# Selection masks split over three engines, a re-ordered sample softmax, and a moved reciprocal in a decoder layer

## The chip, the cores and the metric

The kernel runs on one core of a Trainium2 chip. The metric is the device time of one launch in microseconds (us). The core's engines run beside each other and meet only at semaphores: TensorE (PE in the profile; PEld is its weight loading), VectorE (DVE), ScalarE (ACT), GpSimd (POOL) and SyncE (SP, which only issues DMAs here). Time before: 1739.12 us, the median of 3 runs (1735.95 to 1741.62).

## The reference, cut to what matters

One layer of a decoder for 1024 prompt tokens and 8 sequences of 4 sample tokens, all float32. Mixer A is dilated window attention, mixer B attends to the 256 keys that an indexer picks for each query; then come the output projection, a second normalisation and a SwiGLU FFN.

```python
def select_keys(scores, qpos, topk):            # topk 256 (prompt), 65 (sample)
    causal = jnp.arange(L)[None, :] <= qpos[:, None]
    scores = jnp.where(causal[None], scores, -jnp.inf)
    _, sel = lax.top_k(scores, topk)             # ties: the lowest index first
    return sel, sel <= qpos[None, :, None]
...
    p = jax.nn.softmax(s, axis=-1)               # gathered_attention, mixer B
    o = jnp.einsum('nqkgt,nqtkd->nqkgd', p, vg)
...
def layer_back(x, oa, ob, mods, w_out, norm2_g, w_gate_up, w_down):
    x = x + g1 * (o @ w_out)
    xn = rms_norm(x, norm2_g) * (1 + sc2) + sh2
    gate, up = jnp.split(xn @ w_gate_up, 2, axis=-1)
    return x + g2 * ((jax.nn.silu(gate) * up) @ w_down)
```

## The kernel before

Every engine has its program written out by hand, in four blocks; at a block's end all engines meet, so the engine that ends last sets when the next block starts. Products in float32 are made of three passes over a high and a low part (`gwh`, `gwl` for a weight `gw`; `ahi`, `alo` for an activation): ACT rounds the high part, and POOL or DVE subtracts it for the low one.

**Block 1 (`front`)**: projections of 128-token tiles, on PE. Beside it DVE looks for each query's 256th score by 31 steps of bisection (`count`, `decide`), for six prompt tiles of 384 to 1024 keys (a = 0 to 5) and the sample's 32 x 288 (a = 6). Then `select` makes a tile's mask, 0 where selected and -1e30 elsewhere: `selG` (score above the threshold, with its count), `selE` (equal), a running count of the equal ones in `sig`, `kp` (how many of these are wanted), the equal ones kept (L1466), the sum `selG - 1 + sig` (L1469) and its multiple with 1e30 (L1473, 16 bits for the prompt). POOL's last work there is the low part of the first head's queries and keys (`qst` L1187, `lst` L1190), which PE turns (L693) and ACT copies out (L1043).

**Block 2 (`attention`)**: mixer attention of the prompt, 16 heads.

**Block 3 (`sample_attention`)**: the 32 sample tokens, with sequences in two groups g of four, and x = 0 to 3 for mixer A group 0, A group 1, B group 0, B group 1 (x = g for A, 2 + g for B). PE spreads the sample's mask (L2160) and turns the cached keys `kw` of each sequence n, DVE and ACT copy them, and after each fourth sequence PE makes the scores. Then, one step for all x after another: `smx` and its extreme (L2286, DVE), exponential with row sums `lsum` (L2244, ACT), normalisation by `rsum` (L2290, L2292, DVE), turning (L2203, PE), copies `pT` (L2296, DVE), product with the values `vw` or `vpg` (L2220, PE), picking the head by `headsel` (L2303, L2307, DVE) and a turning product (L2227, PE). SP loads `vw` (8 x 512 KB) after the last `kw`. POOL makes the low part `olo` of the prompt's attention output meanwhile (L2138).

**Block 4 (`back`)**: output projection (L2466), second normalisation in three thirds of 352 tokens (`inverse_root`, `normed`, `normed_low`; ACT makes `ahi`, DVE `alo`), then 11 pairs of FFN slices: `gate_up` (L2489) of two slices f, `down` (L2508). The first `gate_up(0, ...)` takes the thirds as they come; `gate_up(1, ...)` waits for `gwl` of slice 1 (semaphore `gw_lo`).

```python
            for n in range(NSEQ): ...                      # block 3, SP
                sp.dma_start(vw[:, n], ...).then_inc(v_in, 16)
...
            pe.wait_ge(v_in, 16 * NSEQ)                    # block 3, PE
            pe.wait_ge(kv_pg, 2 * 16 * KT * NSEQ)
            pe.wait_ge(pe_, 4)
```

Of the kernel before, what the change touches and what calls it, by code (L numbers as in the profile page):

```python
# [195 lines left out]
def front(nc, A, S):  # L196
# [289 lines left out]
    with nc.Block() as block:  # L486
# [339 lines left out]
        def _(act):  # L826
# [192 lines left out]
            for n in ns:
# [5 lines left out]
                else:  # L1025
# [36 lines left out]
            for a in turns:  # L1062
                ada_bias(a)

        @block.gpsimd
        def _(pool):
# [110 lines left out]
            for q, n in enumerate(ns):  # L1177
                c = proj_no[n]
                for t in range(NTILE + 1):
# [5 lines left out]
                    if u == len(units) - (NTILE + 1) + FIRST_SPLIT_AT:  # L1185
                        pool.wait_ge(S["q_hi"], 1)
# [848 lines left out]
def sample_attention(nc, A, S):  # L2035
# [48 lines left out]
    nr = sem("s_norm_s")  # L2084
# [15 lines left out]
    with nc.Block() as block:  # L2100
# [44 lines left out]
        def _(pe):  # L2145
# [732 lines left out]
```

## Time and profile before

| what | value |
|---|---|
| median of 3 runs | 1739.12 us |
| the profiled execution | 1734.96 us, its span 1733.4 us |
| granted TensorE clock, mean | 0.966 of full speed |
| busy share of the span | PE 92%, DVE 50%, ACT 39%, POOL 35% |
| last work of block 1 | PE 471.87 us, ACT 472.55 us, DVE 478.27 us |
| block 3 | from 784.78 us to 836.08 us |
| block 4's output projection | from 836.55 us |
| first pair's `down` (L2508) | from 998.28 us, PE without a gap from there to 1720.93 us |

A time line's row is: start in us, length in us, engine, line of the kernel, operation, output<-inputs with shapes, how many instructions the row merges (x8), and in brackets how long the engine had been idle before and what ended that. The row of a merged group runs from the first one's start to the last one's end.

### The profile page before, as it was taken

To read this page: it belongs to the slowest core of one execution; us is meant where nothing else is said; L and a number is where in the kernel's file an instruction comes from. 1 tells how busy PE (TensorE), PEld (TensorE's weight loads), DVE (VectorE), ACT (ScalarE), POOL (GpSimd) and SP (SyncE) were. 2 spreads that over 40 slices of the span, in tenths; PEclk is the share of its full clock that TensorE was granted. 3 is DMA by queue.
4 is the path that set the end of the run, shared out by engine and by line. 5 is a ranking of instruction groups with operands and counts; after the bars stand their busy time and mean duration, and the time that the engine had idled before them with its cause. 6 is when DMAs were issued, how large, how long until landed. Compare 5 with 4: busy or idle time off the path is not lost.

```text
span 1733.4 us, 29578 instructions
## 1 busy us (share of the span) xinstructions
PE 1587.4 (92%) x10702; PEld 1485.0 (86%) x10702; DVE 873.5 (50%) x1980; ACT 684.3 (39%) x1788; POOL 605.3 (35%) x758
## 2 busy tenths in 40 slices
PE   4697899999878888886999899999999999999998
PEld 3586688999857777774898899999999999999998
DVE  1804988999958878885215432131330322313315
ACT  4424658788257778773224211112112111020111
POOL 2154167776234324205251423314223233132320
PEclk7799999999979999997999899999999999999999
DMA  8700033535252311007412212111111120111002
GB/s 259 271 25 7 17 111 109 185 111 194 78 160 62 98 37 62 8 1 250 161 37 73 73 37 62 45 28 48 48 49 48 36 60 30 43 48 48 0 1 100
DMA packets 138044, 135.28 MB, mean 78 GB/s; under 512 B 7229, under 2 KB 126957, under 8 KB 137302
## 3 DMA queue, kind: packets, MB, share of 16 engines
q1 hardware_dynamic: 111190, 106.43, 19.5%
q10 hardware_dynamic: 25104, 24.64, 4.4%
q0 software_dynamic: 1648, 2.89, 0.6%
q8 instruction: 58, 0.95, 0.2%
q14 instruction: 44, 0.36, 0.1%
HBM read 115.29 MB, written 27.04 MB: 82 GB/s over the span
## 4 chain that ended last, share of the span: by engine, by line
PE 49%; DVE 2%; ACT 0%; DMA 0%; issue 0%; DVEq 0%; SPq 0%
PE bank L2489 29%; PE wide L2508 15%; PE bank L2466 5%; DVE alo L2756 1%; DMA out_y_p<-yn 0%; DVE xn L2748 0%; DVE rstd L2742 0%; ACT ahi L2600 0%; DVE yn L2817 0%; PE bank L2532 0%; ACT L2576 0%; ACT L2605 0%; DVE x L2720 0%; ACT rstd L2605 0%; DVE x L2797 0%
## 5 line engine op out<-in xcount | busy, mean ns | idle before, releaser
L2712 DVE TENSOR_TENSOR hf<-bank,sg 128x352 f32<-128x352 f32 x66 | 34.6, 525 | 460.6 <-PE bank L2489 447.5
L2669 POOL TENSOR_TENSOR hlo<-hf,hhi 128x352 fp32r<-128x352 f32 x66 | 63.0, 955 | 503.6 <-ACT hhi L2578 503.6
L2489 PE MATMUL bank<-alo,gwh 128*128 128x352 f32 x1056 | 193.9, 326 | 6.9 <-DVE alo L2756 6.9
L2797 DVE SCALAR_TENSOR_TENSOR x<-wide,modT,x 128x352 f32<-128x352 f32 (+1 forms) x264 | 151.3, 573 | 96.8 <-PE wide L2508 96.8
L2489 PE MATMUL bank<-ahi,gwh 128*128 128x352 f32 x1056 | 196.5, 326 | 2.3 <-ACT ahi L2600 1.9
L2489 PE MATMUL bank<-ahi,gwl 128*128 128x352 f32 x1056 | 193.1, 325 | 0.0
L2489 PEld LDWEIGHTS bank<-alo,gwh 128*128 128x128 f32 x1056 | 176.3, 191 | 7.2 <-DVE alo L2756 7.2
L2489 PEld LDWEIGHTS bank<-ahi,gwh 128*128 128x128 f32 x1056 | 175.3, 189 | 6.4 <-ACT ahi L2600 4.8
L2489 PEld LDWEIGHTS bank<-ahi,gwl 128*128 128x128 f32 x1056 | 175.5, 190 | 0.0
L2508 PE MATMUL wide<-hlo,dwh 128*128 128x352 f32 x528 | 171.3, 325 | 0.0
L2576 ACT ACTIVATE sg<-bank 128x352 f32<-128x352 f32 x66 | 30.7, 465 | 354.3 <-PE bank L2489 354.3
L2508 PE MATMUL wide<-hhi,dwl 128*128 128x352 f32 x528 | 170.4, 323 | 0.0
L2508 PE MATMUL wide<-hhi,dwh 128*128 128x352 f32 x528 | 170.0, 322 | 0.0
L2578 ACT ACTIVATE hhi<-hf 128x352 fp32r<-128x352 f32 x66 | 33.0, 500 | 255.7 <-DVE hf L2712 255.7
L2659 POOL TENSOR_TENSOR gwl<-gw,gwh 128x2048 fp32r<-128x2048 f32 x22 | 101.9, 4633 | 48.0 <-ACT gwh L2562 47.9
L1848 PE MATMUL bank<-ident,prob 128*128 128x128 f32 x576 | 97.0, 278 | 17.9 <-DVE pL L1988 16.9
L1988 DVE TENSOR_TENSOR pL<-bank,pH 128x512 fp32r<-128x512 f32 (+1 forms) x192 | 101.4, 551 | 14.5 <-ACT pH L1935 13.1
L1412 DVE TENSOR_SCALAR_CACHE_REDUCE junk<-sig,cand 128x384 uint8<-128x384 f32 (+4 forms) x155 | 106.3, 744 | 0.1
L1960 ACT ACTIVATE prob<-smx,nmax 128x128 f32<-128x128 f32 (+7 forms) x128 | 98.8, 772 | 10.3 <-DVE nmax L2018 9.6
L1935 ACT ACTIVATE pH<-bank 128x512 fp32r<-128x512 f32 (+1 forms) x192 | 90.4, 486 | 25.3 <-PE bank L1848 24.4
L2508 PEld LDWEIGHTS wide<-hhi,dwh 128*128 128x128 f32 x528 | 100.0, 189 | 0.0
L2508 PEld LDWEIGHTS wide<-hlo,dwh 128*128 128x128 f32 x528 | 99.2, 188 | 0.0
(366 smaller groups left out, 3423.1 us busy)
## 6 DMA issues: line engine op xcount, KB each, us to landing
gw<-in_w_gate_up SPq DMA_DIRECT2D x44, 512.0 KB, 5.0
raw<-in_w_ada ACTq DMA_DIRECT2D x14, 1024.0 KB, 8.9
dw<-in_w_down SPq DMA_DIRECT2D x22, 512.0 KB, 3.6
raw<-in_w_ada SPq DMA_DIRECT2D x10, 1024.0 KB, 7.5
raw<-in_w_in ACTq DMA_DIRECT2D x8, 1024.0 KB, 5.7
scr_x<-xT SPq DMA_DIRECT2D x1, 4224.0 KB, 17.5
xnat<-in_x_prompt SPq DMA_DIRECT2D x8, 512.0 KB, 5.6
scr_q<-ubuf SPq DMA_DIRECT2D x32, 128.0 KB, 3.2
```

What stands on the lines that cost most here:

```text
L1412: link(v.tensor_scalar(junk[0:r, joff[a]:joff[a] + w], sig[0:r, o:o + w], cand[0:r, a:a + 1].bitcast(F32), 0.0, ALU.is_ge, ALU.add, accum_ ...
L1848: mm = pe.transpose(dst[:, (j - 4 * b) * P:(j - 4 * b + 1) * P], prob[:, a % RING, j * P:(j + 1) * P], ident[:])
L1935: act.activation(pH[g][:, 4 * b:4 * b + nb, i % 4, :], src[:, 0:nb * P].rearrange("p (j n) -> p j n", n=P), ACT.Copy).then_inc(act_out, 1)
L1960: act.activation(prob[:, m % RING, 0:L], smx[:, m % 2, 0:L], ACT.Exp, scale=-1.0, bias=nmax[:, m % 4:m % 4 + 1], accum_out=rowsum[:, m // ...
L1988: v.tensor_tensor(pL[g][:, 4 * b:4 * b + nb, i % 4, :], src[:, 0:nb * P].rearrange("p (j n) -> p j n", n=P), pH[g][:, 4 * b:4 * b + nb, i ...
L2466: mm = pe.matmul(pb[u % 4][:, 0:THIRD], a[:, d % 2, k, :], b[:, k, third(th)], start=(p == 0 and k == 0), stop=(p == 2 and k == KD - 1))
L2489: mm = pe.matmul(pb[2 * s + side][:, 0:THIRD], a[r][:, k, side, :], b[:, k, third(th)], start=(p == 0 and k == 0), stop=(p == 2 and k == K ...
L2508: mm = pe.matmul(pb[4 + u % 4][:, 0:THIRD], a[:, r, d * P:(d + 1) * P], b[:, r, third(th)], start=(r == 0 and p == 0), stop=(r == 1 and p ...
L2659: pool.tensor_tensor(gwl[r][:], gw[r][:], gwh[r][:].bitcast(F32), ALU.subtract).then_inc(gw_lo, 1)
L2669: pool.tensor_tensor(hlo[:, r, third(th)], hf[:, (3 * r + th) % 2, :], hhi[:, r, third(th)].bitcast(F32), ALU.subtract).then_inc(h_lo, 1)
L2712: v.tensor_tensor(hf[:, s, :], pb[2 * s + 1][:, 0:THIRD], sg[:, s, :], ALU.mult).then_inc(h_mul, 1)
L2797: ins = v.scalar_tensor_tensor(out=x1[:, d, cols], in0=src[:, 0:n], scalar=modT[:, 40 + d, 0:1], in1=x1[:, d, cols], op0=ALU.mult, op1=ALU ...
```

## The change

1. **Selection.** `select` makes `selE` first, then writes the comparison "above the threshold" over the scores `sco`, and computes `kp` after the running count. The sum is left to POOL (`selected`: `sig + sco`, float32), the scaling to ACT (`put_mask`: `1e30 * sig - 1e30`). Three tiles (a = 0, 1, 2) are summed by POOL ahead of its `qst` and `lst`, the four others behind them; ACT writes three masks after its copies of the first head's halves, the four others at its end.
2. **Sample softmax.** The normalisation by `rsum` moves from the probabilities to the output (`scaled`, in the instruction that picks the head). The groups go in the order x = 0, 2, 1, 3; the two of sequences 0 to 3 get their extremes and exponentials between the copies of the later sequences. PE's turning, value products and joining products are issued so that a join stands between value products. The mask is copied by ACT from `wide`, and PE waits for it only at the first scores.
3. **Second normalisation.** `inverse_root(2)` stands ahead of the first third's `hidden` and of `normed_low(1)`; the low part of the second weight slice, `gwl[1]`, is made by DVE after `normed_low(2)` instead of by POOL.

```diff
+            def put_mask(a):
+                r, o, w = (NSAMP if a == 6 else P), ioff[a], width[a]
+                act.wait_ge(pads, 3 + a)
+                dst = mask_sb[:] if a == 6 else mask_b[:, moff[IDXT[a]]:moff[IDXT[a]] + w]
+                act.activation(dst, sig[0:r, o:o + w], ACT.Copy, scale=-NEG, bias=NEG)
...
+                        if u >= len(units) - EARLY_MASKS:
+                            put_mask(u - len(units) + EARLY_MASKS)
...
+            for a in range(EARLY_MASKS, 7):
+                put_mask(a)
...
+            def selected(a):
+                r, o, w = (NSAMP if a == 6 else P), ioff[a], width[a]
+                pool.wait_ge(cand_ready, BITS + 1 + a)
+                pool.tensor_tensor(sig[0:r, o:o + w], sig[0:r, o:o + w], sco[0:r, o:o + w], ALU.add).then_inc(pads, 1)
...
-                link(v.tensor_scalar(selG[0:r, 0:w], sco[0:r, o:o + w], flag[0:r, a:a + 1], 0.0, ALU.is_gt, ALU.add,
-                                     accum_out=cnt[0:r, a:a + 1]))
                 link(v.tensor_scalar(selE[0:r, 0:w], sco[0:r, o:o + w], flag[0:r, a:a + 1], None, ALU.is_equal))
                 joined()
-                link(v.tensor_tensor(kp[0:r, a:a + 1], tk[0:r, 0, a:a + 1], cnt[0:r, a:a + 1], ALU.subtract))
+                link(v.tensor_scalar(sco[0:r, o:o + w], sco[0:r, o:o + w], flag[0:r, a:a + 1], 0.0, ALU.is_gt, ALU.add,
+                                     accum_out=cnt[0:r, a:a + 1]))
                 link(v.tensor_tensor_scan(sig[0:r, o:o + w], selE[0:r, 0:w], selE[0:r, 0:w], 0.0,
                                           ALU.add, ALU.bypass))
                 joined()
-                link(v.scalar_tensor_tensor(out=sig[0:r, o:o + w], in0=sig[0:r, o:o + w], scalar=kp[0:r, a:a + 1],
-                                            in1=selE[0:r, 0:w], op0=ALU.is_le, op1=ALU.mult))
+                link(v.tensor_tensor(kp[0:r, a:a + 1], tk[0:r, 0, a:a + 1], cnt[0:r, a:a + 1], ALU.subtract))
                 joined()
-                link(v.scalar_tensor_tensor(out=sig[0:r, o:o + w], in0=selG[0:r, 0:w], scalar=-1.0,
-                                            in1=sig[0:r, o:o + w], op0=ALU.add, op1=ALU.add))
-                joined()
-                dst = mask_sb[:] if a == 6 else mask_b[:, moff[IDXT[a]]:moff[IDXT[a]] + w]
-                link(v.tensor_scalar(dst, sig[0:r, o:o + w], -NEG, None, ALU.mult))
+                v.scalar_tensor_tensor(out=sig[0:r, o:o + w], in0=sig[0:r, o:o + w], scalar=kp[0:r, a:a + 1],
+                                       in1=selE[0:r, 0:w], op0=ALU.is_le, op1=ALU.mult).then_inc(cand_ready, 1)
+                v.wait_ge(cand_ready, BITS + 1 + a)
...
-            pe.wait_ge(qe, 1)
-            pe.wait_ge(me, 2)
             pe.wait_ge(kv_pg, 16 * KT * NSEQ)
...
+            for q in range(4):
+                turn(q)
+            pe.wait_ge(v_in, 16 * NSEQ)
+            pe.wait_ge(kv_pg, 2 * 16 * KT * NSEQ)
+            weighted(0)
+            weighted(1)
+            weighted(2)
+            join(0)
+            weighted(3)
+            join(1)
+            join(2)
+            join(3)
...
-            for x in range(4):
-                v.wait_ge(ex, x + 1)
-                v.reciprocal(rsum[:, x:x + 1], lsum[:, x:x + 1]).then_inc(rc, 1)
-                v.wait_ge(rc, x + 1)
-                v.tensor_scalar(pr[:, x, :], pr[:, x, :], rsum[:, x:x + 1], None, ALU.mult).then_inc(nr, 1)
...
+                if n in (4, 5):
+                    largest(n - 4)
...
             add_squares(KD - 2)
-            split_gate_up(0, 1)
             pair(0, False)
...
             normed(1, range(KD))
+            v.wait_ge(x1_done, 3 * KD)
+            inverse_root(2)
             hidden(0, 0, True, (0,))
             normed_low(1)
-            v.wait_ge(x1_done, 3 * KD)
-            inverse_root(2)
...
             normed_low(2)
+            v.wait_ge(gw_hi, 2)
+            v.tensor_tensor(gwl[1][:], gw[1][:], gwh[1][:].bitcast(F32), ALU.subtract).then_inc(gw_lo, 1)
```

The instructions as they stand in the engines' rows (the number behind a name tells tensors of one name apart). POOL at the end of block 1, before (`wlo` is a projection weight's low part):

```order
L1125 TENSOR_TENSOR ropeb<-ubuf,rope 32x4x8
L1127 TENSOR_TENSOR ubuf<-ropea,ropeb 32x4x16
L1084 TENSOR_TENSOR wlo<-raw,whi 128x1024 x2
L1187 TENSOR_TENSOR qst_58<-qn_56,qst_58 128x8x64
L1190 TENSOR_TENSOR lst_60<-kn_57,kst_59 128x1024
```

and now:

```order
L1095 TENSOR_TENSOR wlo<-raw,whi 128x1024 x2
L1186 TENSOR_TENSOR sig<-sig,sco 128x384
L1186 TENSOR_TENSOR sig<-sig,sco 128x512
L1186 TENSOR_TENSOR sig<-sig,sco 128x640
L1205 TENSOR_TENSOR qst_58<-qn_56,qst_58 128x8x64
L1208 TENSOR_TENSOR lst_60<-kn_57,kst_59 128x1024
L1186 TENSOR_TENSOR sig<-sig,sco 128x768
L1186 TENSOR_TENSOR sig<-sig,sco 128x896
L1186 TENSOR_TENSOR sig<-sig,sco 128x1024
L1186 TENSOR_TENSOR sig<-sig,sco 32x288
```

Seven sums are new; four stand behind `lst`, last on POOL in this block. DVE in the second normalisation of block 4, before (`rstd` is the root's inverse, `xn` the scaled input):

```order
L2742 RECIPROCAL rstd_13618<-rstd_13618 128x352
L2748 SCALAR_TENSOR_TENSOR xn_13609<-x_13611,sc_13605,rstd_13618 128x352 x8
L2712 TENSOR_TENSOR hf<-bank,sg 128x352
L2756 SCALAR_TENSOR_TENSOR alo<-xn_13609,modT,ahi 128x352 x8
L2742 RECIPROCAL rstd_13618<-rstd_13618 128x352
L2773 TENSOR_TENSOR xn_13609<-x_13611,rstd_13618 128x8x32
L2776 TENSOR_TENSOR xn_13609<-xn_13609,sc_13605 128x8x32
L2779 TENSOR_TENSOR xn_13609<-xn_13609,modT 128x8x32
L2748 SCALAR_TENSOR_TENSOR xn_13609<-x_13611,sc_13605,rstd_13618 128x320 x8
L2783 TENSOR_TENSOR alo<-xn_13609,ahi 128x8x32
L2756 SCALAR_TENSOR_TENSOR alo<-xn_13609,modT,ahi 128x320 x8
```

and now:

```order
L2799 RECIPROCAL rstd_13632<-rstd_13632 128x352
L2805 SCALAR_TENSOR_TENSOR xn_13623<-x_13625,sc_13619,rstd_13632 128x352 x8
L2799 RECIPROCAL rstd_13632<-rstd_13632 128x352
L2769 TENSOR_TENSOR hf<-bank,sg 128x352
L2813 SCALAR_TENSOR_TENSOR alo<-xn_13623,modT,ahi 128x352 x8
L2830 TENSOR_TENSOR xn_13623<-x_13625,rstd_13632 128x8x32
L2833 TENSOR_TENSOR xn_13623<-xn_13623,sc_13619 128x8x32
L2836 TENSOR_TENSOR xn_13623<-xn_13623,modT 128x8x32
L2805 SCALAR_TENSOR_TENSOR xn_13623<-x_13625,sc_13619,rstd_13632 128x320 x8
L2840 TENSOR_TENSOR alo<-xn_13623,ahi 128x8x32
L2813 SCALAR_TENSOR_TENSOR alo<-xn_13623,modT,ahi 128x320 x8
L2844 TENSOR_TENSOR gwl_13631<-gw_13629,gwh_13630 128x2048
```

The third third's reciprocal stands before the `hf` of the first third, and `gwl` is DVE's last instruction of the normalisation.

## Rows read from the trace of the kernel before

**Rows 1.** DVE time line, selection's end: start us, us, instruction, [idle before <-releaser].

```profile
461.68 2.01 DVE L1466 SCALAR_TENSOR_TENSOR sig<-sig,kp,selE 128x896 f32<-128x896 f32 x1
463.72 3.17 DVE L1469 SCALAR_TENSOR_TENSOR sig<-selG,sig 128x896 f32<-128x896 f32 x1
...
473.28 1.22 DVE L1469 SCALAR_TENSOR_TENSOR sig<-selG,sig 128x1024 f32<-128x1024 f32 x1
...
477.97 0.30 DVE L1473 TENSOR_SCALAR mask_sb<-sig 32x288 f32<-32x288 f32 x1
```

**Rows 2.** Groups by line, 0 to 620 us (busy us, mean ns | idle).

```profile
L1469 DVE SCALAR_TENSOR_TENSOR sig<-selG,sig 128x384 f32<-128x384 f32 (+6 forms) x7 | 7.9, 1124 | 0.2
...
L1473 DVE TENSOR_SCALAR mask_b<-sig 128x384 bf16<-128x384 f32 (+5 forms) x6 | 3.2, 527 | 0.2
...
L1462 DVE TENSOR_TENSOR kp<-tk,cnt 128x1 f32<-128x1 f32 (+1 forms) x7 | 1.1, 158 | 0.2
...
L1784 POOL TENSOR_TENSOR lst<-kn,kst 128x1024 fp32r<-128x1024 f32 x8 | 19.1, 2384 | 0.0
```

**Rows 3.** POOL time line, 440 to 480 us.

```profile
460.90 1.83 POOL L1187 TENSOR_TENSOR qst<-qn,qst 128x512 fp32r<-128x512 f32 x1 [23.69 <-ACT qst L1047]
462.69 3.24 POOL L1190 TENSOR_TENSOR lst<-kn,kst 128x1024 fp32r<-128x1024 f32 x1
```

**Rows 4.** ACT time line, 466 to 482 us.

```profile
471.47 1.08 ACT L1043 ACTIVATE kL<-bank 128x512 fp32r<-128x512 f32 x2 [0.20 <-PE bank L693]
```

**Rows 5.** PE time line, sample stage.

```profile
790.78 1.94 PE L2175 MATMUL bank<-ident,kw 128*128 128x128 f32 x8 [2.31 <-DMA vpg<-in_cache_v]
...
818.52 1.54 PE L2203 MATMUL bank<-ident,pr_s 128*128 128x128 f32 x6 [6.53 <-DVE pr_s L2292]
...
822.98 3.29 PE L2220 MATMUL wide<-vw,pT_s 128*32 128x512 f32 x16 [0.90 <-DVE pT_s L2297]
...
831.88 3.74 PE L2227 MATMUL bank<-pick,ob_s 128*128 128x16 f32 x32
```

**Rows 6.** DVE time line, sample stage.

```profile
789.87 0.81 DVE L2271 COPY mask_s<-bank 128x288 f32<-128x288 f32 x2
...
813.38 5.09 DVE L2292 TENSOR_SCALAR pr_s<-pr_s,rsum_s 128x288 f32<-128x288 f32 x1
```

**Rows 7.** Instructions of tile `vw`: count, ns, first and last start; time to landing.

```profile
L2116 SPq DMA_DIRECT2D vw<-in_state_win_v x8: 469/478/824, 803.8 to 807.6; - x8
...
DMA to landing us min/median/max: 5.2/8.8/12.1
```

**Rows 8.** Chain that ended last: start us, us, what.

```profile
951.17 8.97 DVE alo L2756 x8
...
960.18 6.05 PE bank L2489 x19
```

**Rows 9.** DVE time line, second normalisation.

```profile
937.54 4.05 DVE L2756 SCALAR_TENSOR_TENSOR alo<-xn,modT,ahi 128x352 fp32r<-128x352 f32 x8
...
950.73 0.53 DVE L2712 TENSOR_TENSOR hf<-bank,sg 128x352 f32<-128x352 f32 x1 [2.79 <-ACT sg L2576]
...
960.05 2.34 DVE L2742 RECIPROCAL rstd<-rstd 128x352 f32<-128x352 f32 x1
```

**Rows 10.** PE time line, second normalisation.

```profile
974.84 1.46 PE L2489 MATMUL bank<-ahi,gwh 128*128 128x352 f32 x8
```

**Rows 11.** POOL time line, sample stage and second normalisation.

```profile
804.05 14.24 POOL L2138 TENSOR_TENSOR olo<-oT,ahi 128x352 fp32r<-128x352 f32 x16
...
953.68 4.90 POOL L2659 TENSOR_TENSOR gwl<-gw,gwh 128x2048 fp32r<-128x2048 f32 x1 [31.64 <-ACT gwh L2562]
958.54 1.20 POOL L2669 TENSOR_TENSOR hlo<-hf,hhi 128x352 fp32r<-128x352 f32 x1
```

**Rows 12.** Busy us of PE, PEld, DVE, ACT, POOL; granted PE clock, DMA, GB/s.

```profile
824.00:826.00 2.00, 2.00 (x16) 0.26 (x7) 0.00 (x0) 0.04 (x1) 2.00 (x2) 0.55 0.00 0
...
963.00:966.00 3.00, 3.00 (x11) 2.55 (x10) 2.97 (x8) 2.15 (x5) 0.00 (x0) 0.54 0.18 44
```

More of the change, by code:

```diff
@@ L1185, in _ @@
                     if u == len(units) - (NTILE + 1) + FIRST_SPLIT_AT:
+                        for a in range(EARLY_MASKS):
+                            selected(a)
                         pool.wait_ge(S["q_hi"], 1)
@@ L1192, in _ @@
                                            ALU.subtract).then_inc(S["k_lo"], 1)
+            for a in range(EARLY_MASKS, 7):
+                selected(a)
         @block.vector
@@ L2194, in _, with turn @@
                 mm.then_inc(sc, 1)
-            for x in range(4):
-                pe.wait_ge(nr, x + 1)
-                b = bank[x % 2] if x % 2 == 0 else bank[2]
-                if x >= 2:
-                    pe.wait_ge(pe_, x - 1)
+            def turn(q):
+                x = ORDER[q]
+                pe.wait_ge(ex, q + 1)
+                b = bank[2 * (q % 2)]
+                if q >= 2:
+                    pe.wait_ge(pe_, q - 1)
                 for a in range(3):
@@ L2221, in _, with join @@
                 mm.then_inc(om, 1)
-            for x in range(4):
-                pe.wait_ge(oe, x + 1)
+            def join(q):
+                x = ORDER[q]
+                pe.wait_ge(oe, q + 1)
                 for c in range(4):
@@ L2229, in _, with exponential @@
                                    start=True, stop=True)
-            mm.then_inc(xt, 1)
+                if q == 3:
+                    mm.then_inc(xt, 1)
+            for q in range(4):
[10 more added lines that the diff above has]
+            join(3)
         @block.scalar
         def _(act):
+            def exponential(q):
+                x = ORDER[q]
+                act.wait_ge(mx, q + 1)
+                act.activation(pr[:, x, :], smx[:, x, :], ACT.Exp, scale=-1.0, bias=nmax[:, x:x + 1],
+                               accum_out=lsum[:, x:x + 1]).then_inc(ex, 1)
+            for g in range(2):
+                act.wait_ge(mm_m, g + 1)
+                act.activation(mask[:, 2 + g, :], wide[g][:, 0:NEWW], ACT.Copy).then_inc(me, 1)
             for n in range(NSEQ):
@@ L2268, in _, with largest, place, scaled @@
             last.then_inc(ke, 1)
-            for g in range(2):
-                v.wait_ge(mm_m, g + 1)
-                v.tensor_copy(mask[:, 2 + g, :], bank[2 + g][:, 0:NEWW]).then_inc(me, 1)
+            def largest(q):
+                x = ORDER[q]
+                g, c0 = x % 2, 512 * (x // 2)
+                v.wait_ge(sc, 1 + g)
+                if q == 0:
+                    v.wait_ge(ldc, NCONST)
+                    v.wait_ge(small_in, 64)
+                    v.wait_ge(me, 2)
+                v.tensor_tensor_reduce(smx[:, x, :], wide[g][:, c0:c0 + NEWW], mask[:, x, :], -(HD ** -0.5), 3e38,
+                                       ALU.add, ALU.min, nmax[:, x:x + 1]).then_inc(mx, 1)
+            def place(q):
+                x = ORDER[q]
+                v.wait_ge(pt, q + 1)
+                b = bank[2 * (q % 2)]
+                v.tensor_copy(pT[:, x, 0:2, :], b[:, 0:256].rearrange("p (a n) -> p a n", a=2))
+                v.tensor_copy(pT[0:NSAMP, x, 2, :], b[0:NSAMP, 256:384]).then_inc(pe_, 1)
+            def scaled(q):
+                x = ORDER[q]
+                g = x % 2
+                v.wait_ge(rc, 1)
+                v.wait_ge(om, q + 1)
+                if x < 2:
+                    src = wide[g][:, 0:512].rearrange("p (h d) -> p h d", d=HD)
+                    out = ob[:, x, :].rearrange("p (h d) -> p h d", d=HD)
+                    heads = headsel[:].unsqueeze(2).to_broadcast([P, 8, HD])
+                    v.scalar_tensor_tensor(out=out, in0=src, scalar=rsum[:, x:x + 1], in1=heads,
+                                           op0=ALU.mult, op1=ALU.mult).then_inc(oe, 1)
+                else:
+                    for a in range(2):
+                        src = wide[g][:, 512 + HD * a:512 + HD * a + HD].unsqueeze(1).to_broadcast([P, 4, HD])
+                        out = ob[:, x, 256 * a:256 * a + 256].rearrange("p (h d) -> p h d", h=4)
+                        heads = headsel[:, 4 * a:4 * a + 4].unsqueeze(2).to_broadcast([P, 4, HD])
+                        last = v.scalar_tensor_tensor(out=out, in0=src, scalar=rsum[:, x:x + 1], in1=heads,
+                                                      op0=ALU.mult, op1=ALU.mult)
+                    last.then_inc(oe, 1)
             for n in range(NSEQ):
```

62 lines of the change are left out of this document (24 added, 38 removed).

## The prediction

> **What bounds the kernel now.** I read the chain that ended last first. From 836.55 us on it is PE nearly all the way, apart from one stretch: eight DVE instructions at 951.17, 8.97 us long, and then PE's gate products at a slow pace [rows 8]. From 998.28 us to the end PE has no gap, so nothing in the last 735 us can be gained or lost by this change, except at the very start of that stretch. The chain does not show what lies before 836.55, since the four blocks are joined by meetings of all engines; there the time lines at each block's end say who came last. Block 1 ends with DVE at 478.27 us, with the sample's mask [rows 1], some 6 us behind PE and ACT; ACT's last copies end at 472.55 [rows 4]. Block 3 ends with PE's joining product at 835.62 [rows 5], and inside it PE stood 6.53 us before the turning of the probabilities, for DVE's normalisation [rows 5]. So there are three places, and each is worked out from its own rows.
>
> **Part 1, selection.** DVE loses the seven sums of L1469 (7.9 us), the six multiples of L1473 (3.2) and the sample's (0.3): 11.4 us [rows 1, 2]. The seven subtractions of L1462 (1.1 us in all) used to run beside the running count and now stand alone between two waits; I take 0.9. DVE by itself would be done at 478.27 - 11.4 + 0.9 = 467.8. But the block then ends with those who got the work. POOL's price: 2384 ns for 1024 columns [rows 2] is 2.33 ns a column, so 0.9, 1.2 and 1.5 us for the early sums, which fall into POOL's idle time of 23.69 us before `qst` [rows 3], and 1.8, 2.1, 2.4 and 0.7 (7.0 together) for those behind `lst`. ACT's price: two copies of 512 in 1.08 us [rows 4], about 1.05 ns a column, so 3.8 us for the five masks that follow its last copies.
>
> What matters is that the two engines hinder each other. L1466 ended at 463.69, 0.96 us after POOL's `qst` (462.73); L1469 at 466.89, again 0.96 us after POOL's `lst` (465.93); the `lst` itself took 3.24 us instead of 2.38 [rows 1 to 3]. An instruction with two tensors in SBUF on DVE and one on POOL take turns, whole instruction by whole instruction. And turns are not fair: the normalisation of 288 columns at 813.38 lasted 5.09 us, to the end of POOL's sixteen back-to-back subtractions at 818.29 [rows 6, 11]. The Trainium skill ("SBUF — State Buffer", Who interferes with whom) says the same of the port pair that VectorE and GpSimd share: it is locked, and whoever comes second fully blocks until the first instruction ends. The trace agrees, by the two ends 0.96 us behind POOL's.
>
> If they ran freely, POOL would be done at 465.9 + 7.0 = 472.9 and ACT at 472.6 + 3.8 = 476.4: a gain of 1.9. With turns: POOL goes through `lst` and the sums of 768 and 896 columns to about 470.8 while DVE's work on the 1024 tile stands still; DVE needs 1.3 us more for it (1.22 at this width [rows 1]), the 1024 sum takes 2.4 after the sample's comparison (0.3), DVE's sample tile ends 1.5 later, then the last sum (0.7) and mask (0.3), with about 0.4 of semaphores: 477.7. I take that: -0.6 us. Bounds: -1.9 (free) and +1.5 (POOL gets in only when DVE is through at 467.8, pays `qst` and `lst` as well, 1.2 + 2.4 + 7.0 + 0.3, to 478.7, and loses a little more in turns).
>
> **Part 2, sample softmax.** The mask copies (0.81 us, ending at 790.68) leave DVE, and PE's wait before the first `kw` turns ended 0.1 us behind them (the bracket names a DMA, which came earlier) [rows 5, 6]. ACT has nothing else to do there. The loads of later `kw` wait for these turns, so the whole series moves by 0.8, as does SP's list behind it. PE was through with the scores at 818.52 - 6.53 = 811.99, now 811.2. The stall on DVE's 5.09 us goes: DVE writes only PSUM copies there, of the kind that ran beside POOL without loss, and by about 815 all four are turned. What is late next is `vw`: the last of eight loads was issued at 807.6 and the longest landing is 12.1 us [rows 7], 819.7, or 818.9 after the shift. So the value products start at about 818.9 instead of 822.98: -4.0 us. From there PE has the same instructions, 822.98 to 835.62 = 12.6 us; a join costs 3.74 / 4 = 0.9, so joins 1 and 2 cover the scaling of the last output, now two instructions. The reordering among them is worth nothing, as PE waits for none of them.
>
> One price comes back. PE will have idled 4 us before the value products and starts them at the lower of its two clock levels (1.2 GHz). Before, it was there until about 825.8 (0.55 granted in 824 to 826), 2.8 us of that work; after the gap at 960.18 it lasted until about 965.8 (0.54 in 963 to 966), 5.6 us [rows 8, 12]. Half of the difference is lost: 0 to 1.4, I take 0.8. Sum of part 2: -3.2; bounds -4.1 (no loss) and -1.9 (`vw` no earlier, full loss).
>
> **Part 3, second normalisation.** The eight `alo` of the second third took 8.97 us, the same eight of the first 4.05 [rows 8, 9]: the 4.92 lost are POOL's `gwl`, 4.90 us from 953.68 [rows 11]. That POOL work goes. In front of the eight now stands the third reciprocal, 2.34 us, but DVE idled 2.79 there [rows 9]; since it needs ACT's third root, I expect `hf` 0.6 later. What POOL does next, `hlo` (1.2 at most [rows 11], take 1.0), still cuts in: 951.8 + 4.05 + 1.0 = 956.9 instead of 960.14. PE goes on 3.2 earlier, still slow, and the reciprocal no longer stands before the third third. POOL's `dwl` (1024 columns, 2.4) now falls among the third's `alo`, so these end about 968.5, and PE's first slice ends after two more passes at 971.2 (before: 974.84, when the second slice began [rows 10]). DVE's `gwl` of 2048 columns is not in the trace: twice the 1.22 of 1024 [rows 1] is 2.4, to 970.9, and the `hf` behind it frees PE's bank at 971.4. So the second slice starts at about 971.3: -3.5 us. Bounds: -6.3 if PE doesn't fall to the lower clock in the shorter gap and `dwl` comes elsewhere; -1.5 if `gwl` has to wait for one more POOL instruction and PE for it.
>
> **Sum.** -0.6 - 3.2 - 3.5 = -7.3 us. The profiled execution took 1734.96 (span 1733.4), so it would be 1727.7; the median of the three runs stands 4.2 above it, and the forecast is 1739.1 - 7.3 = 1731.8. The difference is 0.42%; what a measurement of this kernel can tell from no change is about 0.3%, 5.2 us.
>
> **Rivals.**
> *Turns eat the gain.* Part 1 ends at its upper bound (+1.5), and in part 3 DVE's new `gwl` loses its turn (-1.5): 1739.1 + 1.5 - 3.2 - 1.5 = 1735.9. For it: the 5.09 us. Against it: DVE's two-tensor work gets shorter in all three places.
> *The loads are the wall.* `w_out`'s two loads are now issued earlier too, behind `vw`; should they share its bandwidth, `vw` lands 2 to 3 us later and part 2 shrinks to -0.6: 1734.4. For it: eight loads landed one after the other in 5.2 to 12.1 us. Against it: they were issued before `vw` was in already, and it still landed by 819.7.
> *More than forecast.* No fall of the clock in part 3, free running in part 1: 1739.1 - 1.9 - 4.1 - 6.3 = 1726.8.
> *Slower: the clock does not come back.* Place: the value products and the first gate products. If PE, after its gaps, stays at 1.2 GHz for as long as the work behind them is broken up by waits, the 9.8 us that ran fast at the end of block 3 (825.8 to 835.6) double, and block 3 ends at 818.9 + 2.8 + 19.6 = 841.3, 5.7 later than before; and the 64 gate products still to come at 956.9 take 6.05 / 19 = 0.318 us each [rows 8], to 977.3, 2.4 later. With part 1: 1739.1 - 0.6 + 5.7 + 2.4 = 1746.6. It decides from the point where the clock is not up by about 831 and 968. For it: the clock stayed down 5.6 us after 960.18. Against it: both times it rose while PE had work without gaps, as it has in the new order.
> *The change doesn't do what it says*: nothing in the order speaks for it.
>
> **How the numbers follow.** Forecast 0.55, more than forecast 0.10, turns 0.15, loads 0.12, clock 0.08. The first two are faster by over 0.3%: 0.65; turns and loads lie within: 0.27; the clock case slower: 0.08. The likeliest case's own range is 1728 to 1735. The range holds the two on the fast side and the two within, with the spread of the three runs at the edges: 1725 to 1738.5.
>
> **What would show it.** Right: block 1 ends with ACT's sample mask, after POOL's last sum, 0 to 2 us before 478.3; PE's first value product waits for `vw`, at 818 to 820, less part 1's gain; no POOL `gwl` beside the second third's `alo`, which take about 5 us; the second slice of `gate_up` starts some 7 us earlier in the span. Wrong: DVE still last in block 1; a value product that waits for `pT`; DVE's `gwl` over 4 us; a stretch of `down` later than 993.

## The result and the profile after

The changed kernel took 1728.78 us (median of six runs, 1725.88 to 1730.94) against 1738.82 us for the kernel before in the same session (six runs, 1735.95 to 1741.62). The ratio is 0.9943, 95% interval 0.9932 to 0.9954: 10.0 us less, between 8.0 and 11.8. Forecast were 7.3 us less. Direction and range held; the three terms of the sum did not, as the rest shows.

The profiled execution of the changed kernel has a span of 1729.3 us, only 4.1 less than the 1733.4 of before: the execution profiled was the slowest of its six (1730.94 us), that of before (1734.96) faster than all six of its own. So I cut both spans at the same instructions: first comparison of the selection, first memset of block 2, first memset of block 3, first `vw` product, first output projection product, first `down` product (before: at 998.12 us; 998.28 is its second), last `down` product, end. The kernel before was profiled a second time for this (see the experiments). All in us, from the time lines:

| stretch | before | before, 2nd profile | after |
|---|---|---|---|
| start to selection | 438.19 | 437.43 | 438.07 |
| selection to block 2 | 41.00 | 41.01 | 41.58 |
| block 2 | 305.59 | 305.52 | 305.73 |
| block 3 to the first `vw` product | 38.19 | 38.20 | 34.01 |
| that product to the output projection | 13.57 | 16.53 | 16.72 |
| output projection to `down` | 161.57 | 161.55 | 156.39 |
| `down` to the last product | 722.80 | 722.80 | 722.80 |
| tail | 12.53 | 12.54 | 14.01 |

Three stretches that differ repeat to 0.02 us in the two profiles of before, and belong to the change: +0.6, -4.2, -5.2, together -8.8. The profiles of the experiments bear the first two out to about 0.2 us (but for the one that moves the loads). The third is less firm: 161.55 to 163.14 us in five profiles with the old second normalisation, 155.70 to 157.15 in seven with the whole new one. The stretch behind the first `vw` product is a matter of the execution: 13.6 or 16.5 us in the *same* kernel. Whether the tail is one too is not shown: it is 13.7 to 14.1 us in four of the six profiles that have parts 2 and 3 together, 12.5 in the other two and in all eight without.

**Selection.** VectorE's time line of the changed kernel (start us, us, instruction): comparisons `selE`, and one that also writes its count.

```profile
440.90 1.34 DVE L1478 TENSOR_SCALAR selE<-sco,flag 128x512 f32<-128x512 f32 x1
...
445.18 1.68 DVE L1478 TENSOR_SCALAR selE<-sco,flag 128x640 f32<-128x640 f32 x1
...
450.34 2.02 DVE L1478 TENSOR_SCALAR selE<-sco,flag 128x768 f32<-128x768 f32 x1
...
456.37 0.69 DVE L1478 TENSOR_SCALAR selE<-sco,flag 128x896 f32<-128x896 f32 x1
...
463.30 1.28 DVE L1480 TENSOR_SCALAR_CACHE_REDUCE sco<-sco,flag 128x1024 f32<-128x1024 f32 x1
...
472.48 2.55 DVE L1478 TENSOR_SCALAR selE<-sco,flag 32x288 f32<-32x288 f32 x1
```

GpSimd's time line there (in brackets the idle time before and who ended it).

```profile
440.94 1.01 POOL L1186 TENSOR_TENSOR sig<-sig,sco 128x384 f32<-128x384 f32 x1 [3.87 <-DVE sig L1487]
445.22 1.29 POOL L1186 TENSOR_TENSOR sig<-sig,sco 128x512 f32<-128x512 f32 x1 [3.27 <-DVE sig L1487]
450.38 1.56 POOL L1186 TENSOR_TENSOR sig<-sig,sco 128x640 f32<-128x640 f32 x1 [3.87 <-DVE sig L1487]
...
465.49 5.88 POOL L1186 TENSOR_TENSOR sig<-sig,sco 128x768 f32<-128x768 f32 x2
472.53 2.35 POOL L1186 TENSOR_TENSOR sig<-sig,sco 128x1024 f32<-128x1024 f32 x1 [1.16 <-DVE sig L1487]
477.05 0.78 POOL L1186 TENSOR_TENSOR sig<-sig,sco 32x288 f32<-32x288 f32 x1 [2.18 <-DVE sig L1487]
479.65 0.20 POOL L1768 MEMSET pH<- 128x128 f32 x1 [1.82 <-POOLq L487]
```

The comparison of 768 columns took 2.02 us with a sum beside it, that of 896 columns 0.69 us with none: each of the three early sums starts 0.04 us behind a comparison, and the comparison ends 0.3 to 0.4 us behind the sum. The prediction had charged turns only to instructions with two tensors in SBUF; this one has one. The Trainium skill ("SBUF — State Buffer", Who interferes with whom) names it: tensor_scalar can take the shared port pair, but not in the form that also writes its accumulator. The trace agrees in both: the counting comparison of 1024 columns beside `lst` took 1.28 us, as in kernels without these sums. Where the Trainium skill there lets whoever issues first go first, the rows show the sum going first though by its row the comparison began 0.04 us earlier.

Beside the late sums VectorE's tile of 1024 columns went slowly: its scan, `kp` and kept equals had taken 2.28, 0.16 and 1.29 us before.

```profile
464.50 3.17 DVE L1482 TENSOR_TENSOR_SCAN sig<-selE 128x1024 f32<-128x1024 f32 x1
467.71 1.63 DVE L1485 TENSOR_TENSOR kp<-tk,cnt 128x1 f32<-128x1 f32 x1
469.37 3.08 DVE L1487 SCALAR_TENSOR_TENSOR sig<-sig,kp,selE 128x1024 f32<-128x1024 f32 x1
```

The last mask comes where the prediction had it, on ACT after the last sum:

```profile
477.86 0.44 ACT L1021 ACTIVATE mask_sb<-sig 32x288 f32<-32x288 f32 x1 [1.90 <-POOL sig L1186]
```

That ends at 478.30, before at 478.27 [rows 1]. But block 2 starts 1.35 us later, not 0.92 as before: the row at 479.65 waited for GpSimd's own sequencer. The instructions at the meeting's line (count, duration ns min/median/max, first and last start) show why: GpSimd's closing DRAIN began at 477.0 and lasted to 479.4, 1.6 us past the end of its last sum.

```profile
L487 POOLq DRAIN  x1: 2385/2385/2385, 477.0 to 477.0; - x1
...
L487 ACTq DRAIN  x1: 459/459/459, 477.9 to 477.9; - x1
```

In the kernel before GpSimd's DRAIN ended as long behind its last work (`lst`, 465.93 us), but far ahead of the meeting, where it cost nothing:

```profile
L486 POOLq DRAIN  x1: 5697/5697/5697, 461.8 to 461.8; - x1
```

**Sample softmax.** PE's time line of the changed kernel, which answers to [rows 5]:

```profile
790.68 1.73 PE L2189 MATMUL bank<-ident,kw 128*128 128x128 f32 x7 [3.25 <-DMA vpg<-in_cache_v]
...
812.95 1.05 PE L2220 MATMUL bank<-ident,pr_s 128*128 128x128 f32 x6 [0.77 <-DVE pT_s L2326]
819.39 3.64 PE L2237 MATMUL wide<-vw,pT_s 128*32 128x512 f32 x16 [5.39 <-DMA vw<-in_state_win_v]
...
826.41 3.08 PE L2237 MATMUL wide<-vw,pT_s 128*32 128x512 f32 x16
```

The wait for DVE's normalisation (6.53 us) is gone, and PE stands before `vw` instead. The value products then run slowly: 3.64 us for 16, which at the higher clock level take 1.92 (in the experiments below). Busy us of PE, PEld, DVE, ACT, POOL, then granted clock, DMA share, GB/s of the changed kernel:

```profile
820.00:828.00 8.00, 8.00 (x56) 1.78 (x52) 1.62 (x3) 2.11 (x2) 4.66 (x2) 0.50 0.10 25
828.00:836.00 8.00, 7.19 (x76) 4.60 (x68) 2.05 (x4) 0.07 (x1) 0.00 (x0) 0.93 0.00 0
```

PE was at its lower level (1.2 GHz) through 8 us without a gap.

**Second normalisation.** VectorE's time line, which answers to [rows 9]:

```profile
948.60 2.35 DVE L2799 RECIPROCAL rstd<-rstd 128x352 f32<-128x352 f32 x1 [1.07 <-ACT rstd L2663]
950.98 0.52 DVE L2769 TENSOR_TENSOR hf<-bank,sg 128x352 f32<-128x352 f32 x1
951.42 4.73 DVE L2813 SCALAR_TENSOR_TENSOR alo<-xn,modT,ahi 128x352 fp32r<-128x352 f32 x8
...
961.36 3.79 DVE L2813 SCALAR_TENSOR_TENSOR alo<-xn,modT,ahi 128x320 fp32r<-128x320 f32 x8
965.07 2.28 DVE L2844 TENSOR_TENSOR gwl<-gw,gwh 128x2048 fp32r<-128x2048 f32 x1
```

GpSimd's, which answers to [rows 11]:

```profile
952.12 1.18 POOL L2727 TENSOR_TENSOR hlo<-hf,hhi 128x352 fp32r<-128x352 f32 x1 [30.50 <-ACT hhi L2636]
962.73 6.89 POOL L2721 TENSOR_TENSOR dwl<-dw,dwh 128x1024 fp32r<-128x1024 f32 x1 [9.44 <-ACT dwh L2626]
```

PE's, which answers to [rows 8, 10]:

```profile
956.21 5.06 PE L2547 MATMUL bank<-alo,gwh 128*128 128x352 f32 x16 [3.41 <-DVE alo L2813]
...
966.63 2.75 PE L2547 MATMUL bank<-alo,gwh 128*128 128x352 f32 x16
969.22 1.46 PE L2547 MATMUL bank<-ahi,gwh 128*128 128x352 f32 x8
```

`alo` of the second third takes 4.73 us instead of 8.97; the second slice starts 5.6 us earlier in the span, 5.2 counted from the output projection: 3.5 of these are the second third's `alo`, 1.7 come behind them. What was to cut into the third third's `alo`, GpSimd's `dwl`, did not: it was the one that waited, 6.89 us, until VectorE's series of eight and the `gwl` behind it were through. PE comes to the third third's `alo` at 966.63, 1.5 us after they are done, and from 956.21 on it waits for nothing. The profile of before had shown `dwl` waiting there already (GpSimd's time line), beside a series of eight that took 3.78 us:

```profile
969.09 4.69 POOL L2663 TENSOR_TENSOR dwl<-dw,dwh 128x1024 fp32r<-128x1024 f32 x1 [9.34 <-ACT dwh L2568]
```

### The profile page after: what moved, and what is told of

It reads as the page before. It is cut to its first block, busy times and chain, and to the rows that moved or that the text cites. A ratio compares the mean times of both kernels' runs of the same rounds, so it can differ in the third digit from the quotient of the medians.

```text
span 1729.3 us, 29588 instructions
## 1 busy us (share of the span) xinstructions
PE 1583.8 (92%) x10702; PEld 1481.2 (86%) x10702; DVE 863.5 (50%) x1960; ACT 688.4 (40%) x1797; POOL 614.5 (36%) x764
## 4 chain that ended last, share of the span: by engine, by line
PE 49%; DVE 1%; DMA 0%; ACT 0%; issue 0%; DVEq 0%; SPq 0%
PE bank L2547 29%; PE wide L2566 15%; PE bank L2524 5%; DVE alo L2813 0%; DMA out_y_p<-yn 0%; DVE rstd L2799 0%; DVE xn L2805 0%; ACT ahi L2658 0%; DVE yn L2876 0%; PE bank L2590 0%; ACT L2663 0%; DVE x L2777 0%; ACT rstd L2663 0%; DVE x L2856 0%; DVE hf L2769 0%
## 5 line engine op out<-in xcount | busy, mean ns | idle before, releaser
L2717 POOL TENSOR_TENSOR gwl<-gw,gwh 128x2048 fp32r<-128x2048 f32 x21 | 97.0, 4619 | 16.4 <-ACT gwh L2620 16.4
L2566 PEld LDWEIGHTS wide<-hhi,dwl 128*128 128x128 f32 x528 | 99.2, 188 | 0.0
```

The source lines that it names most:

```text
L2566: mm = pe.matmul(pb[4 + u % 4][:, 0:THIRD], a[:, r, d * P:(d + 1) * P], b[:, r, third(th)], start=(r == 0 and p == 0), stop=(r == 1 and p ...
L2717: pool.tensor_tensor(gwl[r][:], gw[r][:], gwh[r][:].bitcast(F32), ALU.subtract).then_inc(gw_lo, 1)
```

## The experiments

Each gives the median, the change against the kernel before with its 95% interval, and the stretches of the profile. The change is worked out from the ratio of the runs (the kernel before took 1737.8 to 1739.2 us), and can differ from the difference of two medians by some 2 us.

**One part alone.** The diff of one part applied to the kernel before; its core is in the change above.

> The kernel before with the first part alone (selections written over the scores, sums on GpSimd, 16-bit masks from ScalarE). Theory A (each part is worth what the trace of the changed kernel shows at its place): the first block ends where it did, since GpSimd's three early sums hold VectorE's next comparison up by 0.7 to 1.3 us each; the time is 0.0 to +0.6 us against the kernel before, inside its spread. Theory B (the sums of the forecast): -0.6 us. Rival C (the medians differ by 10.0 us and the traced steps explain 6 to 7, so the first part is worth the rest): -3 to -4 us.

Measured: 1740.53 us, ratio 1.001 (1.0001 to 1.0019): +1.7 us (0.2 to 3.3). Selection 41.58, as in the changed kernel. Theory A is the nearest; B and C fall. The first part does not help; it costs, 0.6 us at its place and at least 0.2 in the whole.

> The kernel before with the second part alone (sample softmax: pipelined by pairs, normalisation folded into the last product). Theory A (the first value product starts when vw has landed, about 3.6 us earlier, but TensorE runs at 1.2 GHz for some 9 us behind the wait instead of 3): the stretch from the block's start to the output projection is 50.7 us long, -1.0 us. Theory B (forecast): the clock is back as fast as before, -3.2 us; the first value product waits for vw in both. Rival C: without the first part's shift the loads land at another time against the scores, and the clock comes back at once: -4 us.

Measured: 1733.36 us, 0.9967 (0.9956 to 0.9979): -5.7 us (-7.7 to -3.7). First `vw` product 34.02 us into the block (-4.2), then 13.92 to the output projection: the loss that theory A took from the profile after belongs to that execution. The clock was back 3.3 us behind the first product here, as theory B has it. A and B fall as sizes; C's size came nearest, but not for its reason (GpSimd's and SP's loads landed where they did).

> The kernel before with the third part alone (second normalisation: reciprocal of the second third before the first product of the feed-forward, last gwl on VectorE). Theory A: -5.2 to -5.6 us, all of it there when the first down product starts (second third's alo beside an idle GpSimd, 4.7 us instead of 9.0). Theory B (forecast): -3.5 us. Rival C: part of it is given back at the end of the program, where the last two stores have to land: -4 us, with the last stores landing in over 4 us.

Measured: 1733.57 us, 0.9968 (0.9955 to 0.9981): -5.6 us (-7.8 to -3.3). Output projection to `down` 157.15 instead of 161.57, although 5.4 us of the projection ran at 1.2 GHz in this execution. Theory A; C falls, the tail is 12.54 us as before.

> The changed kernel with the first part undone (selection as in the kernel before). Theory A (the first part is worth nothing or costs 0.5 us): the time is that of the changed kernel or up to 0.5 us less, -10 us against the kernel before. Theory B (forecast): 0.6 us slower than the changed kernel. Rival C (the first part carries what the trace does not explain): 3 to 4 us slower than the changed kernel, about -6.5 us against the kernel before.

Measured: 1727.01 us, 0.9935 (0.9921 to 0.9949): -11.3 us (-13.7 to -8.9). Selection is 41.00 again, the rest 33.81, 13.80 and 156.39. Theory A: without its first part the change is at least as good. Its interval overlaps that of the whole change; that it is better is shown only by way of the first part's own +1.7.

**Does PE's wait set the clock?** In parts 2 and 3:

```diff
             for q in range(4):
                 turn(q)
+            for i in range(36):
+                pe.transpose(bank[1][:, (i % 2) * P:(i % 2 + 1) * P], ident[:], ident[:])
             pe.wait_ge(v_in, 16 * NSEQ)
```

> Parts 2 and 3, and 36 turns of the identity into a free bank on TensorE while it waits for vw (after the last weights are turned, before the wait). Theory A (block 3 differs between executions, 47.6 to 50.7 us, by how long TensorE stays at 1.2 GHz behind its wait for vw): with no wait of over 1 us ahead of it the granted clock is 1.00 through the value products, the first 16 vw products take 1.9 us instead of 3.4, and block 3 is 45.5 to 46.5 us long, 1.5 us less than the shortest seen; time -12 to -13 us against the kernel before. Rival (the low stretch has its cause in something else, such as the loads at that time or the 32-column products): the clock falls at 815 as before, and nothing or a loss of up to 0.5 us.

Measured: 1727.04 us, 0.9935 (0.9921 to 0.9948): -11.3 us, as without the turns. PE's time line, first in parts 2 and 3 without the turns, then with them:

```profile
819.18 3.42 PE L2221 MATMUL wide<-vw,pT_s 128*32 128x512 f32 x16 [5.35 <-DMA vw<-in_state_win_v]
...
829.21 2.85 PE L2229 MATMUL bank<-pick,ob_s 128*128 128x16 f32 x24
```

```profile
819.32 1.92 PE L2221 MATMUL wide<-vw,pT_s 128*32 128x512 f32 x16 [1.69 <-DMA vw<-in_state_win_v]
...
827.85 4.57 PE L2229 MATMUL bank<-pick,ob_s 128*128 128x16 f32 x24
```

The slow products do come of the wait: with 1.69 us of it left, the first 16 took 1.92 us, as expected; the next run shows the same without turns. But then the clock fell with PE at work (windows of the same run, columns as above):

```profile
820.00:828.00 8.00, 8.00 (x102) 3.02 (x94) 2.38 (x4) 2.11 (x2) 4.68 (x2) 1.00 0.10 25
828.00:836.00 8.00, 7.08 (x33) 7.00 (x34) 3.95 (x11) 2.82 (x8) 0.00 (x0) 0.54 0.23 62
```

The idle 0.92 us in it are the meeting at the block's end. The last joins took 4.57 instead of 2.85 us, and the projection's start ran slowly. The gain of 1.5 us was given back at once; theory A had this half wrong.

**Is `vw`'s landing the wall?** In parts 2 and 3:

```diff
+            for n in range(3):
+                load_values(n)
             for n in range(3, NSEQ):
                 load_window(n)
-            for n in range(NSEQ):
+            for n in range(3, NSEQ):
+                load_values(n)
```

> Parts 2 and 3, and the first three vw loads issued ahead of the fourth kw load, where the loading queue waits for a free kw buffer. Theory A (the landing of vw is the wall of block 3, and the DMA engines had room from 788 to 797): vw has landed by 815 to 816 instead of 818.9, the first value product starts there, the wait is under 2.5 us, and the clock stays up or falls for less: -3 to -5 us against parts 2 and 3, -14 to -16 against the kernel before. Rival (the loads as a whole are the wall: what vw gains kw loses): the last kw lands 2 to 4 us later, the scores end that much later, and the time is that of parts 2 and 3 within 1 us.

Measured: 1728.55 us, 0.995 (0.9931 to 0.9969): -8.7 us (-12.0 to -5.4), no better than without; in the profile the first `vw` product comes 35.17 us into the block instead of 33.81. PE's time line:

```profile
800.41 1.97 PE L2178 MATMUL bank<-ident,kw 128*128 128x128 f32 x8 [4.76 <-DMA kw<-in_state_win_k]
...
819.72 1.92 PE L2226 MATMUL wide<-vw,pT_s 128*32 128x512 f32 x16 [0.88 <-DMA vw<-in_state_win_v]
...
828.26 4.86 PE L2234 MATMUL bank<-pick,ob_s 128*128 128x16 f32 x24
```

The wait moved from `vw` to `kw`; the first value product came no earlier, and behind the short wait the products were fast and the joins slow, as with the turns. The rival comes nearest, but the scores ended 5.8 us later where it had 2 to 4, with a loss of 1.4. That the loads as a whole are the wall is not shown: from 802.84 to 807.97 SyncE issued nothing, since it waited for PE's turns to free a `kw` buffer, and the DMA engines were partly idle (windows, columns as above):

```profile
804.00:807.00 3.00, 3.00 (x43) 1.35 (x33) 0.00 (x0) 0.00 (x0) 3.00 (x4) 0.85 0.62 188
807.00:810.00 3.00, 2.56 (x22) 2.14 (x21) 2.62 (x7) 2.11 (x5) 3.00 (x4) 1.00 0.30 64
```

An order of loads that fills this room was not tried.

**The first part without GpSimd.** On the first part alone:

```diff
-                pool.tensor_tensor(sig[0:r, o:o + w], sig[0:r, o:o + w], sco[0:r, o:o + w], ALU.add).then_inc(pads, 1)
...
                 v.wait_ge(cand_ready, BITS + 1 + a)
+                v.tensor_tensor(sig[0:r, o:o + w], sig[0:r, o:o + w], sco[0:r, o:o + w], ALU.add).then_inc(pads, 1)
```

> The first part with the sums left on VectorE: selections written over the scores, 16-bit masks from ScalarE, nothing added to GpSimd; parts 2 and 3 undone. Theory A (the first part loses what it saves to GpSimd's turns at the port: comparisons of 0.5 to 0.6 us that took 1.3 to 2.0): VectorE's comparisons take 0.48 to 0.62 us again, the seven scalings (3.5 us) are gone, selection ends 2 to 3 us earlier than in the kernel before, less 0.4 us at the block's end that falls on ScalarE; -2 to -3 us. Rival (ScalarE's masks or the end of the block on ScalarE hold it up, not the port): no gain, 0 to +1 us.

VectorE's time line: the comparison that took 1.68 us beside a sum.

```profile
445.56 0.55 DVE L1469 TENSOR_SCALAR selE<-sco,flag 128x640 f32<-128x640 f32 x1
```

Selection to block 2 takes 38.17 us instead of 41.00, and block 2 starts 0.26 us behind ACT's last mask. So 3.4 us between this form and the change's are GpSimd's sums: theory A at its place. They are not lost at the early sums alone: VectorE comes to the tile of 1024 columns at 461.61 us in the changed kernel and at 463.04 here, where it makes the sums itself. The time does not show the gain: 1738.01 us, 0.9999 (0.999 to 1.0009). The other stretches of its profile (305.72, 38.20, 16.48, 161.84) are those of before's second profile. Why the median stays is open.

**The third part, halved.** The reciprocal alone:

```diff
+            v.wait_ge(x1_done, 3 * KD)
+            inverse_root(2)
             hidden(0, 0, True, (0,))
             normed_low(1)
-            v.wait_ge(x1_done, 3 * KD)
-            inverse_root(2)
```

> The third part without its second edit: the reciprocal of the last third moved ahead of the first product, the last gwl left on GpSimd. Theory A (what counts is that GpSimd's gwl no longer lies beside alo of the second third): alo of the second third still takes 8 to 9 us, and the move of the reciprocal gives only what its place is worth; -1 us, from -2 to 0. Rival (the earlier reciprocal lets ScalarE and VectorE run ahead, and is worth most of the 5.2 us): -4 to -5 us.

Measured: 1736.95 us, 0.9988 (0.9979 to 0.9997): -2.1 us (-3.7 to -0.5); projection to `down` 159.85. Theory A, just past its lower end. `alo` is still held by GpSimd's `gwl` (VectorE's row of its time line):

```profile
955.51 8.96 DVE L2756 SCALAR_TENSOR_TENSOR alo<-xn,modT,ahi 128x352 fp32r<-128x352 f32 x8
```

The other half, `gwl` on VectorE alone, without its twin on GpSimd:

```diff
             normed_low(2)
+            v.wait_ge(gw_hi, 2)
+            v.tensor_tensor(gwl[1][:], gw[1][:], gwh[1][:].bitcast(F32), ALU.subtract).then_inc(gw_lo, 1)
```

> The third part without its first edit: the last gwl on VectorE, the reciprocal of the last third where it was. Theory A (the two edits add up: both 5.2 us, the reciprocal alone about 2): alo of the second third takes 4.7 us instead of 9.0, the reciprocal of the last third (2.35 us) follows it, and the time is -3 us, from -4 to -2. Rival (the reciprocal behind alo puts the last third so late that VectorE's own gwl, 2.3 us, is what TensorE waits for): -1 us or less.

Measured: 1734.37 us, 0.9982 (0.9969 to 0.9995): -3.1 us (-5.4 to -0.9); projection to `down` 159.18. Theory A; within their intervals the halves add up, -2.1 and -3.1 to the measured -5.6. By the stretches they are -1.7 and -2.4, 4.1 of the 5.2.

```profile
952.73 4.74 DVE L2755 SCALAR_TENSOR_TENSOR alo<-xn,modT,ahi 128x352 fp32r<-128x352 f32 x8
```

**The kernel before, again**, unchanged.

> The kernel before, unchanged, for a second profile. Theory A (its first profiled execution, 1734.96 us, was a lucky one: block 3 took 51.8 us there and 54.3 to 54.7 in all four profiles of other kernels with the old sample softmax): block 3 takes about 54.4 us, TensorE is at 1.2 GHz from 815 to about 828 and again at the start of the output projection, and the execution is 1737 to 1740 us. Rival (the first profile was typical, and the other kernels' edits lengthen block 3): block 3 takes 51.8 us.

Its execution took 1738.25 us. Theory A: 16.53 us behind the first `vw` product. Windows (columns as above):

```profile
820.00:828.00 8.00, 7.10 (x34) 1.75 (x37) 1.62 (x6) 2.12 (x2) 4.67 (x2) 0.50 0.06 14
828.00:836.00 8.00, 8.00 (x90) 3.60 (x82) 2.50 (x4) 0.00 (x0) 0.00 (x0) 0.80 0.01 2
```

Over all profiles with the old sample softmax this stretch is 13.57 us once and 16.16 to 16.53 six times.

**Towards a better version.** Parts 2 and 3 with the first part in its form without GpSimd (diff above):

> Parts 2 and 3 with the first part in its form without GpSimd (sums on VectorE, masks from ScalarE). Theory A (the 2.3 us by which the second block starts earlier in the trace of that form stay to the end): -13.5 us against the kernel before. Rival (what is gained ahead of block 3 is lost there, since its loads or TensorE's clock then fall differently, as the median of that form alone suggests): -11.3 us, that of parts 2 and 3.

Measured: 1725.78 us, 0.9943 (0.992 to 0.9965): -9.9 us (-13.9 to -6.1). The profiled execution is theory A in each stretch (38.26, 33.91, 13.65, 156.49; span 1722.9), but two of the six runs took 1733 and 1735. The lowest median, undecided by its interval.

Then nine output buffers (VectorE's half; ACT's and SP's lines change alike):

```diff
-                if t >= 3:
-                    v.wait_ge(y_out[t % 3], 16 * (t // 3))
-                v.tensor_copy(yn[0:rows, t % 3, 512:1024], pb[2 * (t % 2) + 1][0:rows, :]).then_inc(y_ev2, 1)
+                v.tensor_copy(yn[0:rows, t, 512:1024], pb[2 * (t % 2) + 1][0:rows, :]).then_inc(y_ev2, 1)
```

> The same, and nine output buffers in place of three, over tiles that are done with by then, so that no copy of the output waits for a store. Theory A (the tail's two waits for stores, 2.7 and 3.0 to 4.8 us, are what lies between the last product and the last store): another -3 to -5 us, from the last product to the last store's issue 5 to 7 us instead of 9.7 to 11.5. Rival (the stores come out at the rate of the queue, and the last one lands as late): 0 to -1 us.

Measured: 1730.56 us, 0.9947 (0.993 to 0.9963): -9.2 us. The last store is issued 7.9 us behind the last product instead of 11.1 in the run before (9.7 in the kernel before), but landed 5.3 us after its issue, not 1.9 (2.2): tail 13.92 us against 13.70, no gain, the rival. This profile also shows the clock of the prediction's slower rival, though not its condition, waits between the products. PE's time line, without a gap from 816.51 to the block's end at 837.68:

```profile
816.51 3.64 PE L2229 MATMUL wide<-vw,pT_s 128*32 128x512 f32 x16 [5.58 <-DMA vw<-in_state_win_v]
...
832.38 5.30 PE L2237 MATMUL bank<-pick,ob_s 128*128 128x16 f32 x24
```

Its windows (columns as above): 1.2 GHz throughout, and the stretch is 22.09 us, 8.4 more than in the run before.

```profile
820.00:828.00 8.00, 8.00 (x60) 1.78 (x56) 1.63 (x3) 0.78 (x1) 4.06 (x2) 0.50 0.01 2
828.00:836.00 8.00, 8.00 (x57) 6.20 (x50) 1.63 (x3) 0.00 (x0) 0.00 (x0) 0.50 0.00 0
```

## Why the prediction was right, and where not

*Part 1: -0.6 forecast, +0.6 at its place, +1.7 (0.2 to 3.3) alone; the sign was wrong.* The last mask was to end at 477.7 and ended at 478.30, and the block ended 0.43 us later still. Two steps failed. I put the early sums into GpSimd's idle time as if they cost VectorE nothing, since I took a comparison with one tensor for free of turns; each held up the next comparison, by 0.9, 1.1 and 1.4 us (1.34, 1.68 and 2.02 against 0.48, 0.55 and 0.61 in the form without GpSimd). A row that I used said otherwise: the normalisation of 5.09 us [rows 6] has the comparison's form, one tensor and a scalar for each partition. How much of these 3.4 us reaches the block's end no run shows. And I ended the block with the last mask; it ends when GpSimd's sequencer has drained, 1.6 us past its last instruction. The times of the late sums came right (VectorE's work on the tile of 1024 columns ended at 472.45, 472.1 forecast), but in part by luck: VectorE did not stand still until GpSimd was through. Its scan went in between `lst` and the sum of 768 columns, which took 3.83 us instead of 1.8.

*Part 2: -3.2 forecast, -5.7 (-7.7 to -3.7) alone.* Its first step held: `vw` bounds, at 819.39 in the changed kernel; -4.0 forecast, -4.2 measured, -4.0 to -4.4 in all six profiles with this order of loads. The step that failed is the price of 0.8 us for the clock, taken as a property of the kernel. It is one of the execution: 13.6 to 16.7 us behind the first product in both kernels, once 22. The execution of before that I worked from was the shortest of seven; the new form was at 13.65 to 13.92 in three profiles of five (the changed kernel, part 2 alone, parts 2 and 3, and the last two), and at 14.03 and 14.32 in the two with turns and with loads moved. That is the likely reason why part 2 alone measures -5.7; so few profiles do not prove a distribution. Of "the loads are the wall" the step was wrong, since `w_out` did not push `vw` back; whether another order of loads would gain more is open.

*Part 3: -3.5 forecast, -5.2 measured.* Right: `gwl` leaves `alo`, `hlo` cuts in (0.7 us, 1.0 forecast), PE goes on 3.5 us earlier (3.2), `gwl` takes 2.28 on VectorE (2.4). Mis-sized is what comes behind: -1.7 measured, -0.3 forecast. `dwl` was charged 2.4 us among the third's `alo`, which took 3.79, as before; VectorE kept its turn, and PE, which was to wait for these `alo`, did not.

*The signs* named came: ACT's mask after GpSimd's last sum (at 478.30, so at the very edge of 0 to 2 us before 478.3), a first value product that waits for `vw` at 819.39, no `gwl` beside `alo`; the second slice is 5.6 us earlier instead of some 7, and `down` at 992.5 just short of the 993 that would have spoken against it.

*Sum.* +0.6 - 4.2 - 5.2 = -8.8 at the places that repeat; -9.6 from the three parts measured alone; -10.0 measured as a whole (8.0 to 11.8). That the forecast's -7.3 came so near is luck: the error of the first part and those of the others have opposite signs.

## What to carry to other kernels

Profile the same kernel twice before a stretch behind a wait of PE goes into a sum: which of its clock levels it got there was worth 3 us and changed from one execution to the next. Work given to GpSimd is not free where VectorE is busy, not even in GpSimd's idle time, and at a block's end its drain counts. When a wait is removed, look for the one behind it: here `vw` stood 4.2 us ahead of the products, and two attempts to get past it, by the clock and by the order of loads, gave nothing.

## What was unexpected of the hardware

- A series of instructions without a pause can hold the other engine up to its end: VectorE's normalisation took 5.09 us, to the end of GpSimd's sixteen subtractions [rows 6, 11], and GpSimd's `dwl` took 6.89 us instead of 2.40 behind a series of VectorE's. It need not: GpSimd's `gwl` before [rows 11] and its `hlo` after (at 952.12) got into the middle of VectorE's eight `alo`. What decides it is not shown.
- Work without gaps did not keep TensorE's clock up, nor bring it back at once. With the turns it fell to 1.2 GHz at 828.7, among the small products of `vnew`, `vpg` and the joins, 9.4 us after the first value product and with no gap since; with the loads moved it fell at 828.8, 9.1 us after. In the last experiment it fell at 814.7, in the wait for `vw`, and stayed down for 27 us, though PE worked from 816.51 on with one gap of 0.92 us at the block's end.
- GpSimd's DRAIN ended 1.6 us after its last instruction; VectorE's, where it came last (parts 2 and 3), 0.7 us, ACT's 0.03 us in the changed kernel.
